# One fp32 two-model kernel on one core: x by halves, exponentials in another order, low halves around additions

## What is computed

```python
    xn = rmsnorm(h, g_mix[l])
    proj = xn @ w_in[l]
    mq, mk, mv, mo, mi, mf, aq, ak, av = jnp.split(proj, split_points, axis=-1)
    ...
    hm = rmsnorm(hm, g_mhead[l].reshape(M_HEADS, M_DV)).reshape(B, S, M_HEADS * M_DV)
    hm = (jax.nn.sigmoid(mo) * hm).astype(x.dtype)
    ha = sliding_window_gqa_sinks(...)
    h = h + jnp.concatenate([hm, ha], axis=-1) @ w_out[l]
    h = h + memory_cross_attention(rmsnorm(h, g_cross[l]), rmsnorm(mem, g_mem[l]), ...)
    h = h + peer_ffn(rmsnorm(h, g_ffn[l]), w_pq[l], sub_keys1[l], sub_keys2[l], ...)
return rmsnorm(h, g_final)
```

```python
    odd:  p = hn @ w_in;  o = gla_chunked(q, k, v, log_alpha)
          return (from_heads(rms_norm(o, out_gain)) * jax.nn.silu(g_r)) @ w_out
```

## Time and profile before

| | before |
|---|---|
| median of 3 runs | 1698.1 us (1697.87 to 1701.24) |
| profiled execution | 1698.76 us |
| its span | 1696.9 us |
| mean granted clock of TensorE | 0.998 |
| PE busy | 1671.6 us, 99%, 12006 instructions |
| DVE busy | 1232.3 us, 73% |
| ACT busy | 951.0 us, 56% |
| POOL busy | 364.7 us, 21% |
| read from HBM | 303.68 MB |

### The profile page before, as it was taken

One profiled execution on the slowest core, in us unless ns is written; L12 is line 12 of the kernel. 1 busy time (PEld: TensorE's weight loads), 2 busy tenths in 40 slices (PEclk: granted clock), 3 DMA queues, 4 the chain that ended last, 5 costly groups with the idle time before them and its releaser, 6 DMA issues.

```text
span 1696.9 us, 30404 instructions
## 1 busy us (share of the span) xinstructions
PE 1671.6 (99%) x12006; PEld 1552.6 (91%) x12006; DVE 1232.3 (73%) x1848; ACT 951.0 (56%) x1182; POOL 364.7 (21%) x417
## 2 busy tenths in 40 slices
PE   8899999999999999999999999999999999999999
PEld 8899999999999999988888887999999788899987
DVE  6775467999998666666666666887788555768873
ACT  7865555545555555544544444785555456555552
POOL 0000000003767776201001000000355000005530
PEclk9999999999999999999999999999999999999999
DMA  8345253676556555777777776533455543345552
GB/s 305 135 146 182 108 177 129 228 237 215 187 179 194 187 187 190 269 243 231 239 239 235 236 241 226 216 125 132 177 190 176 197 173 126 125 174 177 194 190 110
DMA packets 73949, 323.48 MB, mean 191 GB/s; under 512 B 8679, under 2 KB 8935, under 8 KB 55888
## 3 DMA queue, kind: packets, MB, share of 16 engines
q1 hardware_dynamic: 58880, 285.24, 48.9%
q0 software_dynamic: 5568, 19.38, 3.7%
q10 hardware_dynamic: 9360, 16.92, 2.7%
HBM read 303.68 MB, written 17.83 MB: 189 GB/s over the span
## 4 chain that ended last, share of the span: by engine, by line
PE 71%; DVE 14%; issue 5%; ACT 4%; POOL 4%; DMA 1%; POOLq 0%; SPq 0%; DVEq 0%; ACTq 0%
PE bank L602 10%; PE bank L604 10%; PE bank L603 10%; PE bank L982 7%; PE bank L984 7%; PE bank L983 7%; PE bank L935 5%; PE bank L939 5%; PE bank L938 5%; DVE lo_u L2266 3%; DVE wlo L1891 3%; POOL upad L533 3%; PE bank L947 2%; DVE oh L2277 2%; ACT whi L1330 1%
## 5 line engine op out<-in xcount | busy, mean ns | idle before, releaser
L1564 ACT ACTIVATE hi_u<-raw_u 128x1024 fp32r<-128x1024 f32 x256 | 272.0, 1063 | 283.2 <-PE bank L982 167.9
L1891 DVE TENSOR_TENSOR wlo<-raw,whi 128x2048 fp32r<-128x2048 f32 x137 | 314.9, 2298 | 103.9 <-PE bank L602 75.3
L1330 ACT ACTIVATE whi<-raw 128x2048 fp32r<-128x2048 f32 x137 | 262.9, 1919 | 70.1 <-PE bank L602 64.9
L935 PE MATMUL bank<-xh,hi_u 128*128 128x256 f32 x1024 | 292.0, 285 | 1.3 <-DVE lo_u L2266 1.0
L2266 DVE TENSOR_TENSOR lo_u<-raw_u,hi_u 128x1024 fp32r<-128x1024 f32 x192 | 238.3, 1241 | 70.8 <-PE bank L935 62.5
L938 PE MATMUL bank<-xl,hi_u 128*128 128x256 f32 x1024 | 285.6, 279 | 0.0
L939 PE MATMUL bank<-xh,lo_u 128*128 128x256 f32 x1024 | 285.4, 279 | 0.0
L602 PE MATMUL bank<-nh,whi 128*128 128x256 f32 x904 | 256.7, 284 | 1.7 <-DVE wlo L1891 0.9
L497 POOL TENSOR_SCALAR oh<-kept,sel_T 128x128 f32<-128x128 f32 x256 | 198.9, 793 | 254.8 <-ACT sel_T L1614 170.4
L603 PE MATMUL bank<-nl,whi 128*128 128x256 f32 x904 | 252.9, 280 | 0.0
L604 PE MATMUL bank<-nh,wlo 128*128 128x256 f32 x904 | 252.7, 280 | 0.0
(11 more groups left out here) (404 smaller groups left out, 3497.3 us busy)
## 6 DMA issues: line engine op xcount, KB each, us to landing
raw<-in_weights SPq DMA_DIRECT2D x138, 1024.0 KB, 4.8
raw_u<-in_experts SPq DMA_DIRECT2D x256, 512.0 KB, 4.1
aside<-a_out ACTq DMA_DIRECT2D x64, 256.0 KB, 3.4
a_in<-aside POOLq DMA_DIRECT2D x64, 256.0 KB, 3.6
const<-in_const SPq DMA_DIRECT2D x1, 1409.0 KB, 9.8
const<-in_const POOLq DMA_DIRECT2D x1, 1409.0 KB, 6.3
h<-in_x SPq DMA_DIRECT2D x2, 512.0 KB, 5.2
raw<-in_weights SPq DMA_DIRECT2D x4, 256.0 KB, 6.7
```

The lines of the kernel that those rows point to most:

```text
L935: mm = pe.matmul(out, w[0][:, kp], xh[:, k, :], start=(k == 0), stop=False)
L1330: a(A(whi[:, n % HIGH, :], raw[:, n % RAW, :], ACT.Copy), S("weights_hi"))
L1564: a(A(hi_u[:, u % HIGH_U, :], raw_u[:, u % RAW_U, :], ACT.Copy), S("unit_high"))
L1891: v(V.tensor_tensor(wlo[:, n % LOW, :], raw[:, n % RAW, :], whi[:, n % HIGH, :].bitcast(F32), ALU.subtract), S("weights_split"))
```

## The change

The arithmetic stays the same but for one product's order. Seven things move.

1. *Start.* Only the identity (64 KB) is loaded ahead of x; the ones are written by DVE, and iota is loaded behind slot 2. x comes by halves of channels, each for both blocks of tokens, and between the halves come two quarters of slot 0. PE transposes the first half, makes the first 12 products, and then transposes the second half.
2. *First mixer.* On ACT, slot 10's high half and the value drains stand directly behind slot 9's; then come the decays' exponentials, and then those of the window, all of a block in one row. The sigmoid stands behind the drains of `wT`. On DVE, the low halves of slots 11 and 12 stand one step later.
3. *Ends of stages.* Where a residual stage had nothing between its third and last norm pair (`res1`, `res2`, `res4`), the low half of the next slot is made there in two pieces, one on each side of the last pair, and the `point` behind it is gone.
4. *Experts.* The same for slot `BEFORE` around the last low units; its high half one pair of units earlier, behind a wait for the last coefficients; PE transposes for the next norm three products later.
5. *Odd layer.* The second chunk of input weights is multiplied by its high part first, for the first block of tokens, and then by its low part.
6. *ACT behind the third stage.* Two norm pairs stand ahead of the squares.
7. *POOL* multiplies the results of heads 2 and 3 by the gain (four instructions of 128 x 256), DVE does so no longer.

The diff, cut to its core:

```diff
@@ -439,15 +439,16 @@
...
-            sp.dma_start(kept[:, :], t["const"][:, 0:N_KEPT]).then_inc(S("ident_loaded"), 16)
-            for tb in range(TB):
-                sp.dma_start(h[:, tb, :], t["x"][tb * P:(tb + 1) * P, :]).then_inc(S(f"x_loaded{tb}"), 16)
-                if tb == 0:
-                    sp.dma_start(raw[:, 0, QUARTERS[0]], t["weights"][0][:, QUARTERS[0]]).then_inc(S("first_loaded0"), 16)
-            for i in range(1, 4):
-                sp.dma_start(raw[:, 0, QUARTERS[i]], t["weights"][0][:, QUARTERS[i]]).then_inc(S(f"first_loaded{i}") if i < 3 else loaded[0], 16)
+            sp.dma_start(kept[:, 0:P], t["const"][:, 0:P]).then_inc(S("ident_loaded"), 16)
+            for half in range(2):
+                cols_ = slice(half * 512, (half + 1) * 512)
+                for tb in range(TB):
+                    sp.dma_start(h[:, tb, cols_], t["x"][tb * P:(tb + 1) * P, cols_]).then_inc(S(f"x_loaded{half}{tb}"), 16)
+                for i in (2 * half, 2 * half + 1):
+                    sp.dma_start(raw[:, 0, QUARTERS[i]], t["weights"][0][:, QUARTERS[i]]).then_inc(S(f"first_loaded{i}") if i < 3 else loaded[0], 16)
             weights(1)
             weights(2)
+            sp.dma_start(cst("iota"), t["const"][:, CONST["iota"][0]:CONST["iota"][0] + P]).then_inc(S("iota_loaded"), 16)
...
         def _(pool):
+            pool.wait_ge(S("iota_loaded"), 16)
...
+
+            pool.wait_ge(S("gla_means"), 1)
+            for hd in (2, 3):
+                for tb in range(TB):
+                    x = og[:, tb, hd * T:(hd + 1) * T]
+                    pool.tensor_tensor(x, x, row("gla"), ALU.mult).then_inc(S("gla_gained"), 1)
...
-            for tb in range(TB):
-                pe.wait_ge(S(f"x_loaded{tb}"), 16)
...
+            def first_norm(half):
+                for tb in range(TB):
+                    pe.wait_ge(S(f"x_loaded{half}{tb}"), 16)
+                    for k in range(4 * half, 4 * half + 4):
+                        i, c = k // 2, k % 2
+                        mm = pe.transpose(banks[i][:, c * T + tb * P:c * T + (tb + 1) * P], h[:, tb, k * P:(k + 1) * P], ident)
+                        if tb and c:
+                            cur["b"] = of[i]
+                            close(mm)
+
+            first_norm(0)
             bank = open_("w_qk", 0)
+            of_qk = cur["b"]
             for i in range(4):
+                if i == 1:
+                    first_norm(1)
...
+            cur["b"] = of_qk
...
-                        if half + j == 2 and tb == 0:
+                        if half + j + tb == 3:
...
-            odd(1, between=lambda: spread_roots(6))
+
...
+            pe.wait_ge(S("weights_hi"), n + 1)
...
+            for k in range(KD):
+                freeing(pe.matmul(bank[:, 0:T], x_hi[:, k, 0:P], w_hi[:, k, :], start=(k == 0), stop=False))
+                pe.matmul(bank[:, 0:T], x_lo[:, k, 0:P], w_hi[:, k, :], start=False, stop=False)
+            pe.wait_ge(S("weights_split"), n + 1)
+            for k in range(KD):
+                pe.matmul(bank[:, 0:T], x_hi[:, k, 0:P], w_lo[:, k, :], start=False, stop=(k == KD - 1))
+            spread_roots(6)
+            mm = product(bank[:, T:2 * T], (w_hi, w_lo), normed[6], 1)
+            cur["b"] = of
...
             split_hi(9)
+            split_hi(10)
+            values(1)
             def window_exps(tb, hds):
                 for hd in hds:
@@ -1449,15 +1484,12 @@
                     a(A(wS[:, at:at + n], wS[:, at:at + n], ACT.Exp, scale=window_root[:, tb:tb + 1], bias=small[:, 128 + j:129 + j],
                         accum_out=small[:, 144 + j:145 + j]))
+            a(A(mE[:, :, :], mE[:, :, :], ACT.Exp, scale=-1.0), S("mlstm_exp"))
+            a(A(small[:, 80:88], mcol[:, 8:16], ACT.Exp), S("mlstm_exp"))
             act.wait_ge(S("window_max"), 1)
             a(A(small[:, 160:176], small[:, 160:176], ACT.Exp))
             window_exps(0, range(8))
             act.nop().then_inc(S("window_exp"), 1)
-            a(A(mE[:, :, :], mE[:, :, :], ACT.Exp, scale=-1.0), S("mlstm_exp"))
-            a(A(small[:, 80:88], mcol[:, 8:16], ACT.Exp), S("mlstm_exp"))
-            values(1)
-            split_hi(10)
-            window_exps(1, range(3))
             def output_gates(i):
                 bank = full("w_o", i)
@@ -1465,11 +1497,10 @@
             output_gates(0)
             split_hi(11)
-            window_exps(1, range(3, 8))
+            window_exps(1, range(8))
             act.nop().then_inc(S("window_exp"), 1)
             output_gates(1)
             split_hi(12)
-            a(A(mo[:, :, :], mo[:, :, :], ACT.Sigmoid), S("output_gated"))
             for hd in range(4):
                 bank = full("mout", hd)
                 drain(A(mnum[:, hd, :, :], bank[:, 0:2 * (P + 1)].rearrange("p (b d) -> p b d", b=2), ACT.Copy), "mout", hd)
@@ -1478,6 +1509,7 @@
...
+            a(A(mo[:, :, :], mo[:, :, :], ACT.Sigmoid), S("output_gated"))
             split_hi(14)
...
-                    if k == 0 and q + 2 == PAIRS:
+                    if k == 0 and q + 3 == PAIRS:
+
+                        act.wait_ge(S("coef_made"), PAIRS)
                         split_hi(BEFORE)
...
             residual("res2", "even_out", 5)
             ffn(0)
+            for i in range(2):
+                norm_hi(6, i)
             for tb in range(TB):
                 drained("res3", tb)
                 squares(h, tb, 0, 2)
-            for i in range(4):
+            for i in range(2, 4):
                 norm_hi(6, i)
             point(SLOT_OF["odd"])
...
+            def split_lo(n, half=None):
+
+
+                if half != 1:
+                    dve.wait_ge(S("weights_hi"), n + 1)
+                    if n >= LOW:
+                        dve.wait_ge(weights_used, n - LOW + 1)
+                place = slice(0, SLOT) if half is None else slice(half * SLOT // 2, (half + 1) * SLOT // 2)
+                v(V.tensor_tensor(wlo[:, n % LOW, place], raw[:, n % RAW, place], whi[:, n % HIGH, place].bitcast(F32), ALU.subtract),
+                  S("weights_split") if half != 0 else None)
...
@@ -1921,7 +1960,11 @@
                         norm_lo(n, i - 1)
                 if between:
                     between()
-                norm_lo(n, 3)
+                    norm_lo(n, 3)
+                else:
+                    split_lo(SLOT_OF[name] + 5, 0)
+                    norm_lo(n, 3)
+                    split_lo(SLOT_OF[name] + 5, 1)
...
+            v(V.memset(cst("ones"), 1.0))
...
-            split_lo(11)
             def window_normalized(tb):
                 dve.wait_ge(S("window_exp"), tb + 1)
@@ -2057,9 +2100,10 @@
                 by_spread(kxT[:, 2 * i:2 * i + 2, :], full("xk", i), "xk", i, mem_spread)
             window_normalized(0)
-            split_lo(12)
+            split_lo(11)
             memory_keys(0)
             window_normalized(1)
+            split_lo(12)
...
-                point(SLOT_OF["pq"] + i)
-                if i == 0:
+                if i:
+                    point(SLOT_OF["pq"] + i)
+                else:
                     inv_root(3)
-                elif i == 3:
+                if i == 3:
...
+                if q + 1 == PAIRS:
+                    split_lo(BEFORE, 1)
                 unit_lo(P + 2 * q + 1)
                 if q + 2 < PAIRS:
                     coef(q + 2)
                 if q + 1 < PAIRS:
                     coef_low(q + 1)
+                    if q + 2 == PAIRS:
+                        split_lo(BEFORE, 0)
                     unit_lo(P + 2 * q + 2)
-            split_lo(BEFORE)
...
-                point(SLOT_OF[up])
...
+                if hd >= 2:
+                    dve.wait_ge(S("gla_gained"), 2 * hd - 2)
...
-            gained_gate(2)
             mix_lo("gT", 0, 0, 0)
             mix_lo("gT", 1, 0, 1)
-            through_gate(2)
-            gained_gate(3)
-            through_gate(3)
+            for hd in range(2, 4):
+                drained("odd", 8 + hd)
+                through_gate(hd)
```

20 lines of the change are left out of this document (8 added, 12 removed).

## The result

The changed kernel takes 1702.22 us in the median of 15 runs, the kernel before 1698.82 in 15. One run of the changed kernel took 6100.21 us; it counts as slow and is not in the ratio, which goes by the fast runs. The ratio is 1.0017, with an interval of 1.001 to 1.0025: slower by 2.9 us (the two medians lie 3.4 apart), where 3.7 less had been forecast. The profiled execution has a span of 1699.7 us (1696.9 before), PE is busy for 1671.1 us of it (1671.6 before), and it issues the same 12006 instructions. The loss is waiting, and a stretch at the half clock behind one of the waits.

A forecast was written before the change was run, and what follows sets the result against it. PE, busy 99% of the span, was taken to bound the kernel, so only its waits could be won. 1.2 + 3.1 - 1.7 + 0.6 + 0.3 + 0.2 = 3.7 us gave 1694.4 against the median of 1698.1; range 1692.2 to 1697.8.

The forecast's parts named there:

- Start: Kernel's begin: first product at 9.0 instead of 11.32, ACT's slot 1 at 13.9 instead of 15.13; gain 1.2 us.
- 0, if PE is slow: Lower bound of the start's gain: slow first 12 products and 8 transposes take 2.1 us more, which eats the gain.
- First mixer: New order of ACT and DVE removes the 4.0 us stall; gain 3.1 us, bounds 2.4 to 4.4.
- Both caps: First mixer: ACT's drain of transposed probabilities, then DVE's gated heads, limit the gain to 3.1 us.
- res1: End of the second residual stage: signal moves from 231.03 to 232.7, delaying the keys' DMA; loss 1.7 us.
- Issue and transfer move rigidly: End of the second residual stage: the keys' DMA shifts by 1.7, so PE's wait of 0.7 becomes 2.4.
- Rival (a): One new stall, for the keys or in the first mixer, lowers the clock: 1.7 us more, 1696.1; chance 0.20.
- Small edits: Two other stages 0.6, end of the experts 0.3, second layer's mixer 0.2: gain 1.1 us.
- the experts' end: Split halves before the last two low units, additions begin as banks close: gain 0.3 us, between -0.5 and +1.0.
- the second layer's mixer: High product first gains 0, as PE then waits 1.3 for the diagonal; norm pairs ahead of squares give 0.2 us.
- GpSimd's multiplies: Four multiplies taken over from DVE for the last heads: 0, between +0.4 and -0.9 us.
- Rival (c): GpSimd's four multiplies hold DVE up, by up to 3.0 us, 0.9 on PE: 1695.3; chance 0.05.

The follow-up runs named there:

- e14: Changed kernel with its new loads, but all sixteen transposes ahead of the first product as before: 1698.97 us, ratio 1.0001.
- e10: Kernel before with the first mixer's new order of ACT and DVE alone: 1696.86 us, ratio 0.9983.
- e7: Changed kernel, but SP's load of the 1 MB slot waits until the keys have landed: 1699.92 us, ratio 1.0003.
- e8: Changed kernel with the old start (loads and transposes) and the keys' signal ahead of the split's second half at res1: 1695.16 us, ratio 0.9975.
- e15: Changed kernel with all sixteen transposes ahead of the first product, new loads kept, and the end of res1 as before: 1693.48 us, ratio 0.9968.
- e3: Changed kernel with the signal for the keys given ahead of the split's second half at res1: 1698.52 us, ratio 0.9998.
- e9: Changed kernel with the old start (loads and transposes) and the end of res1 as before: 1695.29 us, ratio 0.9974.
- e12: Kernel before with the small edits alone; start, first mixer and res1 as before: 1697.45 us, ratio 0.9989.
- e5: Changed kernel with the first quarter of slot 0 loaded ahead of x, x still by halves: ratio 1.0015.
- e11: Changed kernel with PE's first transposes held until the first half of x of block 0 has landed: 1700.73 us in its one run.
- e13: Changed kernel with the old loads (constants in one piece, x by blocks of tokens) and PE's new order of transposes: 1703.53 us, ratio 1.0024.
- e6: Changed kernel with the constants loaded in one piece of 192 KB ahead of x, x by halves: ratio 1.0012.
- e1: Changed kernel with the old start (constants in one piece, x by blocks of tokens, sixteen transposes first): 1700.17 us, ratio 1.0005.

## Why the prediction was wrong

The range ended at 1697.8, and the sign was wrong. By its own steps:

- **Start, forecast a gain of 1.2, measured a loss of 2.3.** Two terms were mis-sized, both on one chain. The quarter was put at 6.1 from 415 GB/s, a rate read at 11 to 14 us; between 3.5 and 7 the trace of before has 330, the changed kernel's 232, and the quarter came at 8.1. The twelve products were counted at 0.111 us; they took 0.21, the spacing that the earlier trace rows show at the half clock for just that stretch; it stood in a bound and not in the value. That is 2.1 and 1.4 of the 3.6 by which ACT's slot 1 missed its 13.9. The transposes behind them took about the 0.9 that they were given (13.76 to ACT's 14.78). The slow loads alone would have done no harm (e14). It was the order: from the first product on ACT needs the second half's transposes, and these stood behind twelve products at half clock. The bound "0, if PE is slow" was too kind, since it left the time of the first product at its forecast.
- **First mixer, forecast 3.1, measured 3.0** in the trace and 2.9 alone (e10, 1.4 to 4.6 by its interval). Both caps were right, the drain of `wT` (wait 1.7 forecast, 1.7 measured) and the gated heads (1.3 and 1.1). The slow stretch behind the old stall went, and brought nothing beyond the caps, as was said.
- **res1, forecast a loss of 1.7, measured 5.9: 4.0 of waiting and 1.9 of clock.** "Issue and transfer move rigidly" was the false step. The signal was late as forecast (e7: PE waits 2.8). But finishing the split also frees SP's next load, and this queue was not looked at: the split's end moved ahead of the keys' issue, where it had stood 2 us behind it. The time from the keys' issue to PE's product grew from 2.5 to 4.4.
- **Clock.** Rival (a) had 1.7 for one drop, behind a wait of 2.4 or less. It came behind the wait of 4.6, over 6.8 us, and cost 2.4: PE was 3.3 late at the product that waited and 5.7 at 242 us. By 332 us 0.5 of that was back, as it was in e8 and e15, where no clock had fallen there. In eight other profiles with a wait of 4.6 to 5.4 for the keys it fell too, for 3.4 or 6.8 us; with waits of 2.8 (e7), 2.1 (e3) and 1.2 (e8) it didn't. A shorter wait is no safeguard, though: in e15 it fell for 3.4 us from 97.2 on, behind the wait of 1.7 for the drain of `wT`, at which it had held in the changed kernel, e8 and e9. It cost nothing there: from the third slot to the transposes of heads PE won 2.9 as in e8, since the gated heads set the pace.
- **Small edits, forecast 1.1, measured 1.9 alone (e12).** Its interval goes from 0.3 to 3.6, so the timed runs don't tell the two apart, but PE's pairs at the edited places do: res2 gave 0.5, res4 0.6 (0.3 each forecast), the heads that GpSimd multiplies 0.6 (0), the experts' end 0.2 (0.3), the second layer's mixer nothing (0.2), with the wait of 1.5 for the diagonal that was forecast at 1.3. That is 1.9 in the changed kernel and in e12 alike, and at these places nothing above 0.1 in e10, which hasn't the edits. The row of +6.4 in the table above must be read with care: it holds the 0.8 by which, as forecast, the last unit but one starts later, and PE was at +5.6 ahead of it. The other 0.6 of the 2.5 in the table lie where nothing was edited.
- **GpSimd's multiplies, forecast 0, measured a gain of 0.6.** PE's wait of 0.4 for the gated heads went. Rival (c) did happen in part: the four gatings of heads 0 and 1 took 3.25 us beside GpSimd, 2.05 before, and DVE's idle time covered that. One of GpSimd's four took 2.85, where the others, beside these gatings, took 0.92. It began just after DVE's low half of 2.29 us did, at 1471.8, and ended 0.6 us after that half. The Trainium skill, SBUF — State Buffer, section "SBUF: two separate sides", says that one of the two engines holds the shared ports for its whole instruction; this case's trace agrees with it, by the 2.85 and by the 3.25. First the changed kernel's rows, then the one of before:

```profile
1471.74 2.29 DVE L1930 TENSOR_TENSOR wlo<-raw,whi 128x2048 fp32r<-128x2048 f32 x1
...
1474.30 3.25 DVE L2624 SCALAR_TENSOR_TENSOR og<-og,small,ov 128x256 f32<-128x256 f32 x4
...
L555 POOL TENSOR_TENSOR og<-og,rows x4: 915/922/2846, 1471.8 to 1476.4; 128x256 f32<-128x256 f32 x4
```

```profile
1470.24 2.05 DVE L2574 SCALAR_TENSOR_TENSOR og<-og,small,ov 128x256 f32<-128x256 f32 x4
```

In sum: 3.5 wrong at the start and 4.2 at res1, less 0.8 that the small edits gave beyond their forecast and 0.6 that PE won where nothing was edited. That is 6.3 of the 6.6 between -3.7 and +2.9.

## What to carry to other kernels

When a step is moved that signals "done", list every engine that waits on any semaphore of it, SP's loads too, and ask which of them now fires ahead of a transfer that someone waits for; a small urgent DMA must be issued before a large one that isn't urgent. When work is put between two groups of transposes, ask which engine needs the second group and when, not only who needs the first. A stretch that the trace shows at half clock should be costed at half clock if the change leaves the idle time in front of it in place. And time that PE loses ahead of a stage where ACT or DVE sets the pace is not lost: price a slow stretch by what PE waits for next.

## What the runs showed of the hardware

- The first transfers are slow, and more so in this start. The moved bytes from 3.5 to 7.0 us, in the changed kernel and in the kernel before:

```profile
3.50:7.00 3.50, 2.73 (x13) 2.33 (x12) 0.09 (x1) 0.00 (x0) 0.00 (x0) 1.00 0.91 232
```

```profile
3.50:7.00 3.50, 3.06 (x14) 2.71 (x14) 0.17 (x1) 0.60 (x1) 0.00 (x0) 1.00 0.97 330
```

  The DMA engines were nearly as busy in both (0.91 and 0.97). It was 236 with the quarter first (e5), 216 with PE held back (e11), 227 in e14, 307 with the old loads in e13. Over all seventeen profiles, the nine with the identity alone ahead of x have 190 to 280 there and the eight with the 192 KB of constants ahead 289 to 337, whatever the order of the rest. Yet when the first quarter lands doesn't follow from that: with the new loads it was 6.8 to 8.1 behind the identity alone and 7.3 behind the whole constants (e6). Why these transfers are slow is open.
- A small DMA issued behind a large one waited for all of it. In all nine profiles in which SP's load of 1 MB went out with the keys' DMA of 128 KB or up to 0.7 us ahead of it, the keys landed 0.3 us behind that load and took 4.3 to 5.2 us; in the others, with the slot's load later, they took 2.4 to 3.1.
- Seven of the fifteen profiles of experiments, of kernels with either start, have a slow stretch of 3.4 us that begins between 57 and 62 us, that neither the kernel before nor the changed one had in theirs. In e1's PE had not waited ahead of it; it had done the gates' small products on four rows, as it does in the kernel before, where the clock held. By 70 us PE was 1.5 to 1.6 us later for it, but by the transposes of heads at 115 us nothing of this was left in the six that have the new mixer order: they won 3.0 to 3.1 from the third slot to there, the nine without the stretch 2.9 to 3.2.
- Between 330 and 394 us, within the experts, where nothing is edited, PE lost 0.4 us against the kernel before in the changed kernel and 0.8 in e10, nothing in e9 and e11, and won 0.3 in e7, e14 and e15. Nothing was tried on it; half a microsecond in one pair of profiles is no effect of an edit.
